# The last part of a diffusion layer: the second result table added by five accumulating transfers of GpSimd's queue instead of by VectorE

## The reference

```python
hid = silu(einsum('td,edf->tef', xt, w_gate)) * einsum('td,edf->tef', xt, w_up)
hid = hid * combine[..., None]            # two experts per token, weights of the router
out = einsum('tef,efd->td', hid, w_down)
...
x = x + gt2 * hier_moe(h2, lp)            # gt2: a gain per channel
y = rms_norm(x, final_g)
```

## Time and profile before

| | us |
|---|---|
| median of 3 runs | 746.22 |
| lowest, highest | 745.2, 746.88 |
| the profiled execution's own time | 746.89 |
| its span, first to last instruction | 745.2 |
| PE, DVE, ACT, POOL busy in the span | 702.1, 534.5, 411.5, 109.5 |
| the last table loads are issued from | 704.35 |
| last product on TensorE starts | 735.18 |
| last VectorE instruction starts | 740.29 |

### The profile page before, as it was taken

One profiled execution on the slowest core, in us unless ns is written; L12 is line 12 of the kernel. 1 busy time (PEld: TensorE's weight loads), 2 busy tenths in 40 slices (PEclk: granted clock), 3 DMA queues, 4 the chain that ended last, 5 costly groups with the idle time before them and its releaser, 6 DMA issues.

```text
span 745.2 us, 10728 instructions
## 1 busy us (share of the span) xinstructions
PE 702.1 (94%) x3842; PEld 532.2 (71%) x3842; DVE 534.5 (72%) x837; ACT 411.5 (55%) x623; POOL 109.5 (15%) x166
## 2 busy tenths in 40 slices
PE   6889999989999999999999289999999999999994
PEld 2358998949977885555544278888888888888863
DVE  4453716399632135566656989999999999999997
ACT  4755323331233043554543467788888887788833
POOL 3000000000031027554211101111111111111000
PEclk9999999999999999999999599999999999999998
DMA  9991325041399619800039888999999999999663
GB/s 321 416 392 52 121 106 198 22 157 63 142 221 286 228 60 383 224 2 29 29 103 347 290 331 300 365 364 388 373 389 397 382 388 386 376 377 366 235 243 144
DMA packets 81506, 186.26 MB, mean 250 GB/s; under 512 B 9156, under 2 KB 19684, under 8 KB 78260
## 3 DMA queue, kind: packets, MB, share of 16 engines
q1 hardware_dynamic: 73252, 166.64, 61.5%
q0 software_dynamic: 6448, 16.86, 6.7%
q10 hardware_dynamic: 1760, 2.17, 1.0%
HBM read 173.16 MB, written 18.38 MB: 257 GB/s over the span
## 4 chain that ended last, share of the span: by engine, by line
PE 85%; DVE 6%; DMA 4%; ACT 2%; issue 2%; SPq 0%; POOLq 0%; DVEq 0%; ACTq 0%
PE bank L2074 55%; PE bank L1966 13%; PE bank L1975 6%; PE bank L1986 3%; DMA slot<-in_w_ada 2%; PE bank L2235 2%; DMA slot<-in_w_down 2%; PE bank L2213 1%; PE bank L2206 1%; PE bank L2036 1%; DVE big L1904 1%; PE bank L2017 1%; DVE big L1914 1%; DVE big L1909 1%; DMA big<-h_scratch,big 1%
## 5 line engine op out<-in xcount | busy, mean ns | idle before, releaser
L1770 DVE TENSOR_TENSOR WL<-slot,WH 128x1024 fp32r<-128x1024 f32 x188 | 219.2, 1220 | 9.0 <-ACT WH L1223 7.9
L1223 ACT CAST WH<-slot 128x1024 fp32r<-128x1024 f32 x188 | 183.5, 1058 | 2.4 <-PE bank L2074 1.4
L2074 PE MATMUL bank<-WH,xgTh 128*128 128x512 f32 x256 | 102.2, 399 | 3.1 <-DVE xgTl L1762 3.1
L2074 PE MATMUL bank<-hTh,WP 128*128 128x384 f32 (+1 forms) x320 | 99.8, 312 | 1.2 <-DVE hTl L1415 1.2
L2074 PE MATMUL bank<-WH,xgTl 128*128 128x512 f32 x256 | 100.5, 393 | 0.0
L2074 PE MATMUL bank<-hTh,WL 128*128 128x384 f32 (+1 forms) x320 | 98.7, 308 | 0.0
L2074 PE MATMUL bank<-hTl,WP 128*128 128x384 f32 (+1 forms) x320 | 98.7, 308 | 0.0
L2074 PE MATMUL bank<-WL,xgTh 128*128 128x512 f32 x248 | 96.5, 389 | 0.0
L1966 PE MATMUL bank<-slot,big 128*128 128x512 f32 (+1 forms) x224 | 87.7, 539 | 0.1
L1975 PE MATMUL bank<-ident,big 128*128 128x128 f32 x424 | 60.6, 282 | 7.7 <-DMA big<-h_scratch,big 4.8
L1966 PEld LDWEIGHTS bank<-slot,big 128*128 128x128 f32 x224 | 40.9, 190 | 35.1 <-issue 33.1
(11 more groups left out here) (283 smaller groups left out, 1073.4 us busy)
## 6 DMA issues: line engine op xcount, KB each, us to landing
slot<-in_w_down SPq DMA_DIRECT2D x16, 2048.0 KB, 15.5
slot<-in_w_up SPq DMA_DIRECT2D x15, 2048.0 KB, 17.1
slot<-in_w_gate SPq DMA_DIRECT2D x13, 2048.0 KB, 16.0
slot<-in_w_ada SPq DMA_DIRECT2D x12, 2048.0 KB, 11.3
slot<-in_w_in SPq DMA_DIRECT2D x6, 2048.0 KB, 21.2
y_scratch<-dftp SPq DMA_DIRECT2D x1, 5120.0 KB, 35.6
big<-y_scratch SPq DMA_DIRECT2D x10, 512.0 KB, 7.5
slot<-in_w_out SPq DMA_DIRECT2D x2, 2048.0 KB, 15.0
```

The lines of the kernel that those rows point to most:

```text
L1223: act.copy(WH[:, high_half(w, s), r, :], quarter(n, s, w, r)).then_inc(high_ok[w], 1)
L1770: dve.tensor_tensor(quarter_low(n, s, w, r), quarter(n, s, w, r), WH[:, high_half(w, s), r, :].bitcast(F32), ALU.subtract).then_inc(low_ok ...
L2074: ins = pe.matmul(out, l[u], r[v], start=first and i == 0, stop=last and i == 2)
```

## The change

Only the last part changes. SP loads the first half of the table alone, in one transfer of 128 x 5 x 1024 into `yab[:, :, 0]`. GpSimd's queue waits for that whole transfer and then issues five transfers (`add_second_results`), one for each tile, that read the second half of the table and add it to what stands in `yab[:, t, 0]`. Each has a semaphore of its own (`second_in[t]`), and TensorE waits on it before the identity products of tile `t`. `both_results` is gone from VectorE. The branch that isn't taken is changed in the same sense.

```diff
             def load_results():
                 table = y_dram.rearrange("(k t p) n -> p t k n", k=2, p=P)
-                for t in range(NT):
-                    for k in range(2):
-                        sp.dma_start(yab[:, t, k], table[:, t, k]).then_inc(yab_in[t][k], 16)
+                sp.dma_start(yab[:, :, 0], table[:, :, 0]).then_inc(first_in, 16)
...
+            def add_second_results(again):
+
+                table = y_dram.rearrange("(k t p) n -> p t k n", k=2, p=P)
+                pool.wait_ge(first_in, 16 * again + 16)
+                for t in range(NT):
+                    pool.dma_start(yab[:, t, 0], table[:, t, 1], accum_op=ALU.add).then_inc(second_in[t], 16)
             pool.wait_ge(table_zero, 16)
             one_pass(0)
+            add_second_results(0)
...
                 if m == NE and kept(p, m):
                     kept_low(0)
                     selection(1)
-                    for t in range(NT - 1):
-                        both_results(t)
                     kept_low(1)
...
-            def both_results(t):
-                for k in range(2):
-                    dve.wait_ge(yab_in[t][k], 16)
-                dve.tensor_tensor(yab[:, t, 0], yab[:, t, 0], yab[:, t, 1], ALU.add).then_inc(both_ok, 1)
...
                     added(t, again)
-                    if t == 0 and again == 0:
-                        both_results(NT - 1)
-                    elif t > 0:
+                    if t > 0:
                         final_norm(t - 1, again)
...
                     if t >= 3:
                         pe.wait_ge(f_mul, 2 * (again * NT + t - 3) + 2)
-                    pe.wait_ge(both_ok, t + 1)
+                    pe.wait_ge(second_in[t], 16 * again + 16)
```

More of the change, by code:

```diff
@@ L510, in program @@
         y_out = [sem("y_out0"), sem("y_out1")]
-        yab_in = [[sem(f"results_in{t}{k}") for k in range(2)] for t in range(NT)]
-        f_mul, f_sum, both_ok = sem("sum_gated"), sem("sum_full"), sem("results_added")
+        first_in, second_in = sem("first_results_in"), [sem(f"second_results_in{t}") for t in range(NT)]
+        f_mul, f_sum = sem("sum_gated"), sem("sum_full")
         sidx_ok, dest_ok = sem("scatter_idx_ok"), sem("dest_ok")
@@ L930, in _ @@
                 for t in range(NT):
-                    for k in range(2):
-                        pool.wait_ge(yab_in[t][k], 16)
+                    pool.wait_ge(second_in[t], 16)
                 pool.wait_ge(f_sum, 2 * NT)
@@ L940, in _ @@
                 pool.sem_inc(stores_ok, 1)
+                add_second_results(1)
         @block.scalar
@@ L1940, in _ @@
                     for y in (yH[s], yL[s]):
[L1941 to L1946, removed]
+                        ins = dve.tensor_scalar(y[:, :], x[:, 0, :], 0.0, None, ALU.mult)
                 ins.then_inc(selT_ok, 1)
```

## The result

| | before | changed |
|---|---|---|
| median of the runs, us | 746.44 (745.20 to 746.88, 5 runs) | 750.48 (749.22 to 752.34, 5 runs) |
| ratio, 95% interval | | 1.0056 [1.0044, 1.0068] |
| mean span, us | 744.82 (23 other runs) | 748.18 (these 5) |
| device time less span, median, us | 1.74 (the same 23) | 2.55 |

The change costs 4.0 us. The forecast was 746.8, 0.4 us more than before, within 745.0 to 749.9; the time lies outside that range. By the last two rows some 3.4 us of it are in the span and 0.8 outside it, where the prediction had no term at all. The spans of the five runs of before aren't on record, so these rows take 23 later runs of it (median 746.55).

What follows compares the result with a forecast made beforehand. VectorE's adds stall TensorE and VectorE sets the last tiles' pace. Tile 0 starts at 713.4 + 0.1 + 4.6 = 718.1, against 717.55 for no change: +0.55 us, forecast 746.8 us, range 745.0 to 749.9.

Steps and rivals of the forecast that it cites:

- the third term: First adding transfer on GpSimd's queue, issue to landing: 4.6 us, upper bound 6.0.
- the second: GpSimd's wake after the first table lands, some 0.1 us, and its issue of the five adding transfers, 2.8 to 5.2 us.
- The stall of 1.04 us: TensorE's wait before tile 0's selection product, put down to VectorE's adds; forecast to disappear.
- the train: From tile 1's gating to the last store: fixed sequence, 3.86 us a tile, so a shift there moves the end equally.
- X: Time TensorE starts tile 0's identity products: 716.12 before, forecast 718.1; tile 1 is gated 6.89 us later.
- The ceiling: Most the change could win in the last part, with tile 0's start unmoved: 1.43 us.
- The half rate of an add: Skill page's rule that an add in a DMA engine needs two source reads, so its stream moves at half a copy's rate.
- The add's surplus: Extra time of the first adding transfer over a plain one: 1.3 us for another passage, 0.3 for issue.
- the plain base, 3.0: Plain 512 KB transfer from issue to landing, 3.0 us, taken from GpSimd's plain stores.
- The prediction's own sign of being wrong: First add landing outside 717.2 to 719.0; also TensorE waiting before a later tile, or a period other than 3.86 us.
- The clock rival: TensorE's clock falls in the idle gap before tile 0; end up to 3.5 us later, 750; chance 0.05.
- My own case: TensorE starts tile 0 between 717.2 and 719.0, giving 745.9 to 747.7 us; chance 0.50.

Runs made afterwards that it cites:

- without the second table the padded kernel: Kernel before with the second table neither loaded nor added, plus ten VectorE adds in the untaken branch; ratio 0.9985.
- tile by tile: Changed kernel with the first table loaded by five transfers, a semaphore each, and ten VectorE adds more in the untaken branch; 745.64 us, ratio 0.9982.
- the six profiles: All six profiles of the changed kernel, with or without ten dead VectorE adds; load issue to TensorE's tile 0 took 14.60 to 14.91 us.
- the profile after: First profile of the changed kernel, against the profile of before; TensorE started tile 0 at 720.24 and tile 1 was gated at 728.86.
- The padded kernel: Changed kernel with ten adds more on VectorE in the branch that isn't taken; ratio 1.0033.
- the three extra profiles: Three more profiles of the changed kernel with ten dead VectorE adds, nothing else changed; spans of 745.8, 746.1 and 746.9 us.
- the second set: The changed kernel run once more, unaltered, against before; 749.70 us, ratio 1.0041.
- the unpadded nine-product kernel: Changed kernel with nine idle products on TensorE before tile 0's identity products, without dead adds; 749.77 us, ratio 1.0038.
- its two shorter forms: Kernel before with five or ten instructions fewer in VectorE's untaken branch; ratio 1.0001 each.

## Why the prediction was wrong, by its own steps

The step of the sum that failed is the third term, with the second: the first adding transfer was given 0.1 + 4.6 us and took 0.3 + 5.4. Beside it the difference between device time and span, which the forecast carried over unchanged, grew by 0.8 us, and the fall of the clock, priced at a chance of 0.05, came in the first profile. The rest is open.

**What held.** The stall of 1.04 us went; the wait on a transfer took its place; no later tile waits; the train is fixed from the gating of tile 1; it comes at X + 6.87 to X + 7.03 wherever the clock stays (forecast 6.89). The ceiling is of the right size: without the second table the padded kernel wins 0.92 us of span, tile by tile 1.23, though 1.43 was the most of three profiles. The first table landed 8.8 to 9.0 us after its issue, and the adds came 2.8 us apart (forecast 2.6), under TensorE's 3.57. The half rate of an add, weighed there as a rule, is what the traces show.

**Terms 2 and 3 were too small by 1.0 us.** Forecast were 0.1 + 4.6. Measured were 0.3 + 5.4. The add's surplus was right; the plain base, 3.0, was read off stores at another place (2.9 lowest, 3.2 in the middle), where a load of the table lands in 3.8 to 4.0. The mean of the six profiles is 14.74 for 13.75, which puts X near 719.1 and the loss near 1.5 us. The prediction's own sign of being wrong was a first add that lands outside 717.2 to 719.0: it landed at 720.10 in the profile after, at 719.2 in one other, and inside in four of six. By itself this step gives 747.8 us and doesn't leave the range.

**The clock rival had too small a chance.** It was seen in one of six profiles, where it took 1.73 us (the forecast said up to 3.5). Averaged it is 0.3 us. The trace of before held evidence for more: a gap of 2.54 us at 151 with a fall behind it, and one of 1.90 at 442.7 without. The profile after has it the other way round at both places, so behind such gaps a fall comes in one execution and not in the next.

**A term was missing.** 0.8 us of the 4.0 lie outside the span. The prediction took the difference between time and span as fixed; the edit of the program moved it from 1.74 to 2.55, and ten dead instructions moved it back to 1.73.

**The sum now.** Gating of tile 1 in the five profiles without the fall is 725.55 in the mean, +1.15 us against before; with the fall in one of six +1.4; outside the span +0.8: +2.2 us. The two sets of runs show +4.0 and +3.2. The padded kernel's spans with the three extra profiles, fifteen in all, lie 1.9 us above those of before, where the profiles give 1.4. So 0.5 us in the padded kernel, and 1.0 to 1.8 in the others, stay without a cause that was shown. Without this open part the time would have been within the range, and the second set's median of 749.70 is within it too, so the range was missed by little. The tile-by-tile kernel, without the wait, has lost this part too: 3.34 us of span for a gating 2.5 us earlier. So it goes with the wait on the chain; why the wait costs more than itself isn't shown. Two long executions were profiled: the first profile, with the clock down in the gap and at 444, and the unpadded nine-product kernel, with the clock down at 444 and a late load, but not at tile 0. The mean clock of each run points the same way: of the fifteen padded ones the seven with spans of 747.5 or more have 0.9796 in the mean, the seven of 746.2 or less 0.9816. That is a correlation in figures rounded to 0.001, and it doesn't say at which place the clock fell.

**The range.** My own case, 745.9 to 747.7, was made of X alone. Every rival was priced as if it came by itself, while here a chain 1.0 us too long, a fall of the clock and a shift outside the span came in the same direction together. Their sum, 0.4 + 1.0 + 1.7 + 0.8 = 3.9 us over the median of before, 750.3 us, is what a range for this change had to reach; even that is just short of the measured 750.48.

## What to carry to other kernels

When work is taken from an engine and given to a chain of transfers, look at what the chain waits for before its price: here one semaphore for five tiles made TensorE wait some 2 us, and with one for each tile the same adds were wholly hidden and the kernel was the fastest of all with a full result. A change that can win 1.4 us at most shouldn't open an idle gap of 2 us ahead of TensorE, since the granted clock may then take another 1.7. And before a difference of under a microsecond is put down to the work, look at the time outside the span and try the same kernel with some dead instructions more.

## What the runs showed of the hardware

- An adding transfer of 512 KB from GpSimd's queue is issued in 0.99 us at first (1.30 in one of six profiles) and up to 2.48 when others are before it, a plain one in 0.54 to 0.58. The first lands after 5.2 to 5.6 us, with the DMA engines idle at its issue (plain 3.8 to 4.0), and the five move at 197 to 215 GB/s against 320 to 430.
- GpSimd adds 128 x 1024 float32 in 2.9 us, and while it does VectorE's operations from SBUF take 2.3 to 4.5 times as long (2.35 to 6.05 for two, 0.55 to 1.26 and 2.50), those with an operand in a bank no longer (1.28).
- After the same idle time of TensorE the granted clock falls to 0.50 in one execution and stays at 1.00 in another: 1.90 us at 442.7 (fell after, stayed before), 2.54 at 151 (fell before, stayed after), and ahead of tile 0 a fall at 2.19 and none at 1.51 to 2.43 in five others. At 3.54 us ahead of tile 0 it fell.
- The time outside the span differs by 0.8 to 1.0 us between programs that do the same on the chip and differ in dead code alone (changed kernel, padded or not); between before and its two shorter forms it differs by 0.03.
